# The recurrent gates' weights as granules of the projection's ring, multiplied in three passes of high and low parts

## The reference, cut to what matters

```python
def block_diag_linear(x, w, bias):
    b, s, _ = x.shape
    xb = x.reshape(b, s, RNN_BLOCKS, RNN_BLOCK_W)             # 8 blocks of 256
    return jnp.einsum('bsni,nij->bsnj', xb, w).reshape(b, s, D_RNN) + bias

def rg_lru(x, w_a, b_a, w_i, b_i, lam, reverse):
    r = jax.nn.sigmoid(block_diag_linear(x, w_a, b_a))
    i = jax.nn.sigmoid(block_diag_linear(x, w_i, b_i))
    log_a = -LRU_C * r * jax.nn.softplus(-lam)
    a = jnp.exp(log_a)
    u = jnp.sqrt(-jnp.expm1(2.0 * log_a)) * (i * x)
    # hs[t] = a[t] * hs[t-1] + u[t], forwards or backwards in time
    ...

def recurrent_mixer(h, w_in, conv_w, conv_b, w_a, b_a, w_i, b_i, lam, w_out):
    xb, yb = jnp.split(h @ w_in, 2, axis=-1)                  # [256, 2048] @ [2048, 4096]
    yb = jax.nn.gelu(yb, approximate=True)
    xb = depthwise_conv_centred(xb, conv_w, conv_b)           # 4 taps over time
    h_fwd = rg_lru(xb, w_a[0], b_a[0], w_i[0], b_i[0], lam[0], reverse=False)
    h_bwd = rg_lru(xb, w_a[1], b_a[1], w_i[1], b_i[1], lam[1], reverse=True)
    return ((h_fwd + h_bwd) * yb) @ w_out
```

## Time and profile before

| what | value |
|---|---|
| median of 3 runs | 3035.77 us (3035.71 to 3037.69) |
| the profiled execution | 3033.72 us |
| its span in the profile | 3032.1 us |
| TensorE busy | 3024.7 us, 100% of the span |
| VectorE, ScalarE busy | 1712.5 us (56%), 1546.5 us (51%) |
| the stage of the change | about 1988 to 2219 us of the span |

### The profile page before, as it was taken

The page is one execution under the profiler, slowest core; times in us unless marked ns, Lnnn a source line. Parts: engine busy times, 40 slices in busy tenths (PEclk is TensorE's granted clock), DMA queues, the critical chain, the costliest instruction groups (busy, mean ns, idle before and its releaser), DMA issues.

```text
span 3032.1 us, 37463 instructions
## 1 busy us (share of the span) xinstructions
PE 3024.7 (100%) x14305; PEld 2532.1 (84%) x14305; DVE 1712.5 (56%) x2011; ACT 1546.5 (51%) x2125; POOL 299.9 (10%) x252
## 2 busy tenths in 40 slices
PE   9999999999999999999999999999999999999999
PEld 8888888988888888888888888888888888888887
DVE  5666655589555675544444455568855444444554
ACT  5556554555654664544444444467845444444443
POOL 1043200145000450000000000001000000000000
PEclk9999999999999999999999999999999999999999
DMA  9674335555445544555655555565455556555554
GB/s 312 199 234 154 129 128 180 164 184 175 139 157 190 181 152 140 185 190 181 197 189 180 195 193 193 190 201 178 140 200 188 183 185 199 184 183 196 192 192 151
DMA packets 256721, 551.84 MB, mean 182 GB/s; under 512 B 9728, under 2 KB 43264, under 8 KB 245856
## 3 DMA queue, kind: packets, MB, share of 16 engines
q1 hardware_dynamic: 255824, 548.79, 54.5%
q0 software_dynamic: 752, 1.48, 0.2%
q10 hardware_dynamic: 32, 0.01, 0.0%
HBM read 548.14 MB, written 2.10 MB: 181 GB/s over the span
## 4 chain that ended last, share of the span: by engine, by line
PE 98%; DVE 1%; ACT 0%; DMA 0%; issue 0%; SPq 0%
PE psum L734 42%; PE psum L2364 32%; PE psum L2502 16%; PE psum L2640 2%; PE psum L1462 2%; PE psum L1478 1%; PE psum L976 1%; PE psum L1490 1%; PE psum L2333 1%; PE psum L1451 1%; PE psum L2091 0%; DVE weights_lo L550 0%; PE psum L1686 0%; PE psum L1962 0%; PE psum L1465 0%; DMA proj<-in_mem 0%
## 5 line engine op out<-in xcount | busy, mean ns | idle before, releaser
L550 DVE TENSOR_TENSOR weights_lo<-weights,weights_hi 128x1024 fp32r<-128x1024 f32 (+2 forms) x1015 | 1259.1, 1251 | 1018.0 <-ACT weights_hi L532 1016.4
L532 ACT ACTIVATE weights_hi<-weights 128x1024 fp32r<-128x1024 f32 (+2 forms) x1015 | 1052.1, 1047 | 1200.2 <-PE psum L734 549.4
L734 PE MATMUL psum<-weights_hi,act_hi 128*128 128x512 f32 (+3 forms) x1952 | 764.3, 392 | 0.3 <-DVE weights_lo L550 0.2
L734 PE MATMUL psum<-weights_hi,act_lo 128*128 128x512 f32 (+3 forms) x1952 | 749.1, 384 | 0.0
L734 PE MATMUL psum<-weights_lo,act_hi 128*128 128x512 f32 (+3 forms) x1952 | 748.1, 383 | 0.0
L2364 PE MATMUL psum<-weights_hi,act_hi 128*128 128x512 f32 x1408 | 549.8, 391 | 0.0
L2364 PE MATMUL psum<-weights_hi,act_lo 128*128 128x512 f32 x1408 | 548.1, 389 | 0.0
L2364 PE MATMUL psum<-weights_lo,act_hi 128*128 128x512 f32 x1408 | 547.8, 389 | 0.0
L734 PEld LDWEIGHTS psum<-weights_hi,act_hi 128*128 128x128 f32 x1952 | 366.7, 188 | 69.1 <-issue 4.6
L734 PEld LDWEIGHTS psum<-weights_hi,act_lo 128*128 128x128 f32 x1952 | 366.3, 188 | 68.0
L734 PEld LDWEIGHTS psum<-weights_lo,act_hi 128*128 128x128 f32 x1952 | 367.2, 188 | 62.9
(11 more groups left out here) (262 smaller groups left out, 1921.3 us busy)
## 6 DMA issues: line engine op xcount, KB each, us to landing
weights<-in_ffn_w_gate SPq DMA_DIRECT2D x88, 1024.0 KB, 5.1
weights<-in_ffn_w_up SPq DMA_DIRECT2D x88, 1024.0 KB, 5.1
weights<-in_ffn_w_down SPq DMA_DIRECT2D x88, 1024.0 KB, 4.8
weights<-in_odd_w_in SPq DMA_DIRECT2D x40, 1024.0 KB, 5.1
weights<-in_even_w_in SPq DMA_DIRECT2D x36, 1024.0 KB, 5.0
weights<-in_w_out SPq DMA_DIRECT2D x32, 1024.0 KB, 5.0
weights<-in_rnn_w_in SPq DMA_DIRECT2D x32, 1024.0 KB, 5.3
weights<-in_attn_w_qkv SPq DMA_DIRECT2D x24, 1024.0 KB, 5.2
```

Source lines behind the costliest of these rows:

```text
L532: e.nc.scalar.activation(e.WH[(2 * slot + b) % HL][:, 0:n // 2], e.RAW[slot][:, b * n // 2:(b + 1) * n // 2], ACT.Copy).then_inc(self.hi.s ...
L550: e.nc.vector.tensor_tensor(e.WL[s][:, 0:n // 2], e.RAW[slot][:, b * n // 2:(b + 1) * n // 2], e.WH[s][:, 0:n // 2].bitcast(F32), ALU.subt ...
L734: last = e.nc.tensor.matmul(e.PS[:, banks.start + m, 0:w], a, x, start=(kk == 0 and n == 0), stop=(kk == KT - 1 and n == 2))
```

## The change

The gates' weights of a block become a granule of the ring. `GatedGemm`, a new kind of `Gemm`, lists 32 + 8 items; a gate granule n stands behind the projection's granule s for which `GATES` names it. Each such item is loaded into a ring slot, split by ScalarE and VectorE as any other granule, and multiplied from its two halves (one for each kind of gate). The convolved input of a block is split too, into `XH` (ScalarE) and `XL` (VectorE), two buffers each, in the memory that the gate weights had. `GATES` moves from the distances 2 and 3 to 3 and 4, so TensorE's order becomes M9, transposes, M10, M11, M12, G2, M13, G3, M14. The units of a block are multiplied and read in another order (both directions of one kind of gate first).

```diff
-        e.GW = [take(f"rnn_weights{s}", [P, GRAN], F32, off)[0] for s, off in enumerate((p_off + 8192 + 12288 * RING, g_off))]
+        e.XH, e.XL = ([take(f"rnn_conv_{part}{s}", [P, 2, T], F32R, off + s * 2048)[0] for s in range(2)]
+                      for part, off in (("hi", p_off + 8192 + 12288 * RING), ("lo", g_off)))
...
-        flow.add(Gemm, evac="xy", prep=Norm(e, e.X[:], GC_MIX + KT, lead=HALF_LEAD), beside=rnn)
+        flow.add(GatedGemm, evac="xy", prep=Norm(e, e.X[:], GC_MIX + KT, lead=HALF_LEAD), beside=rnn)
...
+class GatedGemm(Gemm):
+    GATES = RNN_BLOCKS
+    def __init__(self, e, prev, evac, prep, beside):
+        super().__init__(e, prev, evac, prep, None, beside)
+        self.items = []
+        for s, at in enumerate(self.order):
+            self.items.append((s, at, None))
+            self.items += [(s, None, n) for n in beside.blocks(s, beside.GATES)]
+        self.done = {at[0]: i for i, (s, at, n) in enumerate(self.items) if n is None}
+        beside.use(self, {n: i for i, (s, at, n) in enumerate(self.items) if n is not None})
+
+    def sync(self, sp):
+        e = self.e
+        for i, (s, at, n) in enumerate(self.items):
...
+            sp.wait_ge(e.s_lo.sem, (self.g0 + i - RAW + 1) * 2)
+            for part, (w, d) in enumerate((w, d) for w in e.gate_weights for d in range(2)):
+                done = e.s_gw if part < 3 else e.s_load[i % 4]
+                sp.dma_start(e.RAW[i % 4][:, part * 512:(part + 1) * 512].rearrange("p (i j) -> p i j", i=2),
+                             w[d, n].rearrange("(i p) j -> p i j", p=P)).then_inc(done.sem, 16)
+
+    def scalar(self, act):
+        prep = self.prep
+        for i, (s, at, n) in enumerate(self.items):
+            if n is not None:
+                act.wait_ge(self.beside.gw.sem, self.beside.gw.at(3 * n + 3))
+                self.split_hi(act, i, i % 4, i // 4 + 1)
+                for done in self.finished(i):
+                    self.evacuate(act, done)
+                continue
...
+    def tensor(self, pe):
+        e, prep = self.e, self.prep
+        prep.before_tensor(pe)
+        for i, (s, at, n) in enumerate(self.items):
+            if n is not None:
+                for b in range(2):
+                    pe.wait_ge(self.lo.sem, self.lo.at(2 * i + b + 1))
+                    wh, wl = (x[(2 * i + b) % HL][:].rearrange("p (d i j) -> p d i j", d=2, i=2) for x in (e.WH, e.WL))
+                    self.beside.gates(pe, n, b, wh, wl).then_inc(self.used.sem, 1)
+                continue
...
-    CONV, GATES, SIGMOID, DECAY, ROOT, SCAN = 2, (2, 3), (4, 5), (6, 7), 8, (9, 10)
+    CONV, GATES, SIGMOID, DECAY, ROOT, SCAN = 2, (3, 4), (4, 5), (6, 7), 8, (9, 10)
...
+    def gates(self, pe, n, typ, wh, wl):
+        e = self.e
+        pe.wait_ge(self.xlo.sem, self.xlo.at(n + 1))
+        xh, xl = e.XH[n % 2], e.XL[n % 2]
+        for d in range(2):
+            u = 2 * typ + d
...
+            for j in range(2):
+                out, cols = e.PS[:, self.UNIT_BANK[u], j * T:(j + 1) * T], slice(j * P, (j + 1) * P)
+                for i in range(2):
+                    for k, (w, x) in enumerate(passes(wh[:, d, i, cols], wl[:, d, i, cols], xh[:, i, :], xl[:, i, :])):
+                        last = e.nc.tensor.matmul(out, w, x, start=(i == 0 and k == 0), stop=(i == 1 and k == 2))
+        return last
...
+        for n in self.blocks(s, self.GATES):
+            act.wait_ge(self.conv.sem, self.conv.at(n + 1))
+            if n >= 2:
+                act.wait_ge(*self.multiplied(n - 2, 1))
+            nc.scalar.activation(e.XH[n % 2][:], e.XC[:, 2 * n:2 * n + 2, :], ACT.Copy).then_inc(self.xhi.sem, 1)
...
-                d, typ = u // 2, u % 2
-                act.wait_ge(self.score.sem, self.score.at(4 * n + u + 1))
+                typ, d = u // 2, u % 2
+                act.wait_ge(*self.multiplied(n, typ))
...
+        for n in self.blocks(s, self.GATES):
+            dve.wait_ge(self.xhi.sem, self.xhi.at(n + 1))
+            nc.vector.tensor_tensor(e.XL[n % 2][:], e.XC[:, 2 * n:2 * n + 2, :], e.XH[n % 2][:].bitcast(F32),
+                                    ALU.subtract).then_inc(self.xlo.sem, 1)
```

More of the change, by code:

```diff
@@ L332, in build @@
         e.s_gated = Signal(ctx, nc, "s_gated")
-        e.s_gw = [Signal(ctx, nc, f"s_gate_weights{s}", 16) for s in range(2)]
+        e.s_gw = Signal(ctx, nc, "s_gate_weights", 16)
+        e.s_xhi = Signal(ctx, nc, "s_conv_hi")
+        e.s_xlo = Signal(ctx, nc, "s_conv_lo")
         e.s_const = Signal(ctx, nc, "s_const", 16)
@@ L2566, in __init__, with use, multiplied @@
         self.e = e
-        self.turned, self.centre, self.conv, self.score, self.sigmoid, self.input, self.decay, self.radicand, self.rooted, \
+        self.turned, self.centre, self.conv, self.xhi, self.xlo, self.sigmoid, self.input, self.decay, self.radicand, self.rooted, \
             self.scanned, self.summed, self.rates, self.evac, self.square = (
-                s.mark() for s in (e.s_stage_a, e.s_centre, e.s_conv, e.s_score, e.s_sigmoid, e.s_input, e.s_decay, e.s_radicand,
+                s.mark() for s in (e.s_stage_a, e.s_centre, e.s_conv, e.s_xhi, e.s_xlo, e.s_sigmoid, e.s_input, e.s_decay, e.s_radicand,
                                    e.s_rooted, e.s_scanned, e.s_summed, e.s_rates, e.s_evac, e.s_square))
-        self.gw = [s.mark() for s in e.s_gw]
+        self.gw = e.s_gw.mark()
+    def use(self, proj, granules):
+        self.proj, self.granules = proj, granules
+    def multiplied(self, n, half):
+        return self.proj.used.sem, self.proj.used.at(2 * self.granules[n] + half + 1)
     def between(self, dve, s):
@@ L2598 @@
     rate = lambda self, r, d, k: self.e.RP[:, r, d * KT + k:d * KT + k + 1]
[L2600 to L2607, removed]
-                             w[d, n].rearrange("(i p) j -> p i j", p=P)).then_inc(self.gw[n % 2].sem, 16)
     def tensor(self, pe, s):
@@ L2624, in tensor @@
             last.then_inc(self.turned.sem, 1)
[L2625 to L2642 removed]
+    def gates(self, pe, n, typ, wh, wl):
[4 more added lines that the diff above has]
+            u = 2 * typ + d
+            if n % 2 == 0 and u == 2:
+                pe.wait_ge(self.conv.sem, self.conv.at(n + 2))
+            if n >= 1:
+                pe.wait_ge(self.sigmoid.sem, self.sigmoid.at(4 * n - 4 + u + 1))
+            for j in range(2):
[4 more added lines that the diff above has]
+        return last
     def scalar(self, act, s):
@@ L2738, in pool @@
             for d in range(2):
-                pool.wait_ge(self.sigmoid.sem, self.sigmoid.at(4 * n + 2 * d + 2))
+                pool.wait_ge(self.sigmoid.sem, self.sigmoid.at(4 * n + 2 + d + 1))
                 u = e.RIX[n % RING][:, d]
```

83 lines of the change are left out of this document (64 added, 19 removed).

## The result

Median 3045.75 us (3044.82 to 3047.06, 8 runs) against 3035.74 us (3034.27 to 3037.69, 8 runs) of the kernel before: ratio 1.0033, 95% interval 1.0022 to 1.0044. The kernel is 10 us slower. The forecast was 3043.4 and the range 3033 to 3052.

A forecast was written before the change was run, and what follows sets the result against it. TensorE, busy 3024.7 of 3032.1 us, was taken as the bound. Gates -8.5, stalls +3.8 +3.8 +5.6 +0.5 and one clock fall +2.4 gave +7.6: 3033.72 became 3041.3, and 3043.4 on the median; range 3033 to 3052.

The forecast's parts named there:

- The gates: TensorE's gate blocks: 48 float32r matmuls 0.122 us apart, 5.85 us a block instead of 6.91, saving 8.5 us.
- The line through 512 and 368 columns: Gate matmul pace drawn from two measured float32r widths: 0.41 ns a column, 0.122 us at 256 columns.
- The dear bounds: Gate matmuls: float32 pace 10.4 us a block, 28 us lost; weight-load rival 9.1 a block, 3069 us, chance 0.08.
- The rule that the prediction took from the Trainium skill: Gate matmul pace N / 2.4 + 2.5 ns: 0.109 us at 256 columns, saving 13.4 us; not adopted.
- The stalls: TensorE stands still 3.8 us before M12, 3.8 before M17, 5.6 before M22, and 0.5 behind the last pair.
- The chain from G1's end to M12: ScalarE's, then VectorE's work before M12 takes 21.0 us against TensorE's 17.2, so TensorE waits 3.8 us.
- the rival without a stall: VectorE reaches M12, M17 and M22 before TensorE, given 3.8 us of slack: 3027.3 us, chance 0.07.
- no break through taps and decays: Sign in the changed profile: VectorE works without a break before each of TensorE's three waits of 3 to 6 us.
- one fall: TensorE's clock falls only behind the 5.6 us gap before M22, costing 2.4 us (bounds 0 and 3.6).
- the clock falls at all three gaps: Rival: TensorE's clock also falls behind both 3.8 us gaps, twice 2.4 us more: 3048.2 us, chance 0.15.
- The gap between the profiled execution and the median: Whole kernel: the runs' median of 3035.77 us lies 2.0 above the profiled 3033.72, added to the forecast.

The follow-up runs named there:

- order alone: The kernel before with only the gates' distances moved from 2 and 3 to 3 and 4, gates still float32 and unsplit: 3051.95 us, ratio 1.0053.
- all squares moved: Changed kernel with recurrent steps reordered and scans in two parts, plus ScalarE instead of VectorE squaring all decays: 3041.1 us.
- the version without the gates' low parts: Changed kernel, VectorE making only 16 columns of each gate low split, TensorE using the high part instead: 3045.58 us.
- half of them moved: Changed kernel with recurrent steps reordered and scans in two parts, plus ScalarE squaring only the even blocks' decays: 3037.63 us.
- new gates, old order: Changed kernel with the gates' distances put back to 2 and 3, float32r gates still granules of the ring: 3062.1 us, ratio 1.0092.

## Why the prediction was right

**The gates.** Forecast 0.122 us a matmul and 8.5 us saved. Measured 0.118 us, 5.65 us a block, and 10.2 saved. Of the difference, 8 x 0.20 = 1.6 us is the pace. The line through 512 and 368 columns bends a little below them. The dear bounds (bound by the weight load, paced like a float32 pass) are refuted. The rule that the prediction took from the Trainium skill (TensorE: Matmul & The Clock Gate, Back-to-back issue gap) is given there for an isolated matmul, not for a stream of them. It makes 0.109 us of 256 columns, where this stream shows 0.118.

**The stalls.** Forecast 3.8, 3.8, 5.6 and 0.5; measured 3.72, 3.63, 5.42 and 0.39. The chain from G1's end to M12 was put at 21.0 us and took 2055.96 - 2034.82 = 21.14. Link by link it is the chain that was forecast: ScalarE's four activations, M10's split, the table load and the eight decay instructions, then VectorE's queue. The order alone gave stalls at the same places, 0.7 us shorter each; the relief of VectorE from gate splits changed none of them. That they arise from the move is shown. That there was no slack of 3.8 us anywhere, on which the rival without a stall hung, follows too. VectorE had no break through taps and decays, as forecast. Nothing but M26 waited besides the three, for 0.39 us.

**The clock: the step that failed.** I put one fall in, behind the longest gap, because the earlier trace rows show an idle TensorE for 4.15 us at a granted 1.00. All three gaps were followed by one, and a gap of 1.77 us (all squares moved, clock 0.50 from 2071.90 to 2075.30) and one of 3.00 (order alone, 0.51) as well, though other gaps of that size were not (see the last section). That row was of the span's end, where no work came behind the gap, so it could show neither a fall nor its price. The price was well bracketed: 2.9, 1.7 and 2.6 us, forecast 2.4. The term was 2.4 for one fall where 7.2 was measured. The sum by its terms: forecast -8.5 + 13.7 + 2.4 = +7.6, measured -10.2 + 13.8 + 7.2 = +10.8 (stalls with their hand-over). So what happened is the rival "the clock falls at all three gaps", with cheaper gates. The stage came out 3.2 us above the forecast sum because the errors of +4.8 and -1.7 partly cancel, and that is luck. The median misses by 2.4 instead, because the medians differ by 10.0 us where the two profiled stages differ by 11.1. The Trainium skill (TensorE: Matmul & The Clock Gate, The HAM clock gate) says that idleness lowers the clock; the rows behind these gaps agree, with 0.427 instead of 0.227 us a matmul.

**The gap between the profiled execution and the median.** I added 2.0 us for it. The last section has a likely source.

## What to carry to other kernels

Where one engine is the bound, price a reordering by the chain that leads to each place where it takes over work, not by the busy shares: 3.0 us of wait ahead of M12 came from an order with no instruction added. Count, behind every new gap on TensorE of the size seen here (3.6 to 5.4 us), what the matmuls after it lose at half pace: 1.7 to 2.9 us in the changed kernel, and 1.5 behind the same gap of 3.72 in the version without the gates' low parts. And where two helpers are each busy for 85 to 93% of the period, moving work from one to the other brought no gain in either of two tries; of what was built on that order, only less work helped.

## What the runs showed of the hardware

- A gap is not all that decides whether the clock falls. In the traces of the changed kernel and the experiments, each of the 19 gaps of 3.3 us or more in this stage was followed by a fall; of 18 gaps from 1.7 to 3.2 us ten were and eight were not. 1.77 us did it with all squares moved and did not with half of them moved (clock 1.00 from 2068.84 to 2074.00). The longest that did not are 2.92 (order alone) and 3.13 (new gates, old order); the windows behind these two:

```profile
2107.43:2113.00 5.57, 5.57 (x24) 4.61 (x25) 4.94 (x6) 2.59 (x4) 0.00 (x0) 1.00 0.60 187
```

```profile
2108.72:2114.50 5.78, 5.78 (x48) 5.78 (x49) 3.95 (x4) 5.75 (x9) 0.00 (x0) 1.00 0.61 194
```

  What tells them apart stays open.
- A fall near 215 us of the span, far ahead of the change, is in the trace of the changed kernel and in nine of the twelve experiments'. In the profiled execution of before and in the other three it is not. There many small matmuls of 15 columns run; the window and two rows of TensorE's timeline (after):

```profile
212.00:222.00 10.00, 10.00 (x59) 9.60 (x57) 4.21 (x9) 3.58 (x5) 3.50 (x5) 0.83 0.78 266
```

```profile
212.27 3.89 PE L1831 MATMUL psum<-cmp_k_t,proj 128*128 128x15 f32 x32
...
216.49 0.55 PE L739 MATMUL psum<-weights_lo,act_hi 128*128 128x416 f32 x1
```

  In the kernel before the same window has 1.00 and 416 columns start 0.19 us apart, here 0.35. It costs about 2 us, the distance of that profiled execution (3033.72) from its median. The mean granted clock of an execution fits this: of 106 executions of the kernel before that were timed beside the experiments, 27 have 1.000 and took 3034.0 to 3035.4 us, 71 have 0.999 and took 3035.0 to 3038.4, and 8 have 0.998 and took 3038.5 to 3041.1. Where in the span these lost their clock was not recorded, so that the median's executions have this very fall is likely and not shown.
- GpSimd stretches VectorE: two scans of 128x256 take 1.27 us alone and 3.29 beside two GpSimd products. In this stage of all fourteen traces, the 34 pairs of scans that took 2.2 to 3.4 us all ran beside a GpSimd product; the 164 pairs with no product beside them, and 26 that a product overlapped only in part, took 1.27 or 1.28.
